# WKV inversion in packed 128x64 tiles, and in-step tiles kept in the conv layer's down products only

## The reference

```python
def step(state, inp):                       # wkv7_scan, 16 heads of 64, in both directions
    r_t, w_t, k_t, v_t, a_t, b_t = inp
    sa = einsum('bhvk,bhk->bhv', state, a_t)
    state = state * w_t[:, :, None, :] + sa[..., None] * b_t[:, :, None, :] + v_t[..., None] * k_t[:, :, None, :]
    y = einsum('bhvk,bhk->bhv', state, r_t)
    return state, y

def conv_ffn(h, w_up, conv_w, conv_b, w_down):
    u = h @ w_up                            # 1024 -> 2 * 2816
    acc = conv of width 3 over tokens
    gate, val = split(acc, 2)
    return (silu(gate) * val) @ w_down      # 2816 -> 1024
```

## Time and profile before

| | |
|---|---|
| median of three runs | 3595.13 us (3588.78 to 3596.03) |
| the profiled execution | 3587.22 us, span 3585.4 us, mean granted clock of TensorE 0.951 |
| TensorE busy | 3249.8 us, 91% of the span, 21000 matmul records |
| TensorE weight loads | 2580.9 us, 72% |
| VectorE busy | 2053.4 us, 57% |
| ScalarE busy | 1455.9 us, 41% |
| POOL busy | 725.8 us, 20% |
| DMA | 260.79 MB, 73 GB/s |

### The profile page before, as it was taken

One profiled execution on the slowest core, in us unless ns is written; L12 is line 12 of the kernel. 1 busy time (PEld: TensorE's weight loads), 2 busy tenths in 40 slices (PEclk: granted clock), 3 DMA queues, 4 the chain that ended last, 5 costly groups with the idle time before them and its releaser, 6 DMA issues. The chain is left out here.

```text
span 3585.4 us, 51130 instructions
## 1 busy us (share of the span) xinstructions
PE 3249.8 (91%) x21000; PEld 2580.9 (72%) x21000; DVE 2053.4 (57%) x2984; ACT 1455.9 (41%) x2418; POOL 725.8 (20%) x496
## 2 busy tenths in 40 slices
PE   8888999989878999989899997996888888889999
PEld 6656787868556888866588875765777777768887
DVE  6665634355764524356657375536677777547454
ACT  5444322234454212334644242445455544334332
POOL 1000302120001302020011012315454455201010
PEclk9999999999889999989999998997999999889999
DMA  4101333322003333320133232442000000023232
GB/s 144 41 1 65 106 95 93 99 71 88 10 8 99 95 95 94 95 71 7 48 96 105 83 96 79 156 173 69 22 25 25 25 25 34 7 88 100 95 93 84
DMA packets 82311, 260.79 MB, mean 73 GB/s; under 512 B 9632, under 2 KB 13216, under 8 KB 81696
## 3 DMA queue, kind: packets, MB, share of 16 engines
q1 hardware_dynamic: 71424, 236.02, 20.9%
q10 hardware_dynamic: 10656, 21.50, 1.6%
HBM read 236.51 MB, written 20.97 MB: 72 GB/s over the span
## 5 line engine op out<-in xcount | busy, mean ns | idle before, releaser
L1634 DVE TENSOR_TENSOR mlp_w_lo<-mlp_ring,mlp_w_hi 128x1024 fp32r<-128x1024 f32 (+1 forms) x211 | 251.6, 1193 | 616.9 <-ACT mlp_w_hi L1614 616.7
L1614 ACT ACTIVATE mlp_w_hi<-mlp_ring 128x1024 fp32r<-128x1024 f32 (+1 forms) x211 | 213.0, 1010 | 707.9 <-PE ps L1575 700.8
L1634 DVE TENSOR_TENSOR ffn_w_lo<-ffn_ring,ffn_w_hi 128x1024 fp32r<-128x1024 f32 (+3 forms) x172 | 225.7, 1312 | 459.8 <-ACT ffn_w_hi L1614 459.8
L1614 ACT ACTIVATE ffn_w_hi<-ffn_ring 128x1024 fp32r<-128x1024 f32 (+3 forms) x172 | 186.9, 1088 | 493.8 <-PE ps L1575 487.5
L1574 PE MATMUL ps<-mlp_more_parts,mlp_w_hi 128*128 128x512 f32 x952 | 377.5, 397 | 0.0
L1573 PE MATMUL ps<-mlp_more_parts,mlp_w_hi 128*128 128x512 f32 x760 | 312.1, 411 | 44.0 <-DVE mlp_w_lo L1634 29.1
L1573 PE MATMUL ps<-tiles_parts,mlp_w_hi 128*128 128x512 f32 x832 | 330.5, 397 | 8.0 <-issue 5.7
L1573 PE MATMUL ps<-ffn_x_parts,ffn_w_hi 128*128 128x512 f32 x792 | 312.7, 395 | 26.3 <-DVE ffn_x_parts L2344 20.9
L1575 PE MATMUL ps<-tiles_parts,mlp_w_lo 128*128 128x512 f32 x832 | 328.2, 394 | 0.0
L1574 PE MATMUL ps<-ffn_x_parts,ffn_w_hi 128*128 128x512 f32 x792 | 309.9, 391 | 0.0
L1575 PE MATMUL ps<-ffn_x_parts,ffn_w_lo 128*128 128x512 f32 x792 | 309.8, 391 | 0.0
(11 more groups left out here) (494 smaller groups left out, 6857.2 us busy)
## 6 DMA issues: line engine op xcount, KB each, us to landing
ffn_ring<-in_w_ffn_up SPq DMA_DIRECT2D x88, 512.0 KB, 3.5
mlp_ring<-in_w_up SPq DMA_DIRECT2D x64, 512.0 KB, 3.5
mlp_ring<-in_w_down SPq DMA_DIRECT2D x64, 512.0 KB, 3.5
rwkv_keep<-ffn_ring ACTq DMA_DIRECT2D x64, 256.0 KB, 2.5
sq<-rwkv_keep SPq DMA_DIRECT2D x64, 256.0 KB, 2.9
ffn_ring<-in_w_ffn_down SPq DMA_DIRECT2D x16, 768.0 KB, 4.3
in_ring<-in_w_in SPq DMA_DIRECT2D x22, 512.0 KB, 3.5
mlp_ring<-in_w_in SPq DMA_DIRECT2D x22, 512.0 KB, 3.5
```

Of the source, the lines that this page charges most:

```text
L1614: nc.scalar.activation(w.w_hi[:, n % SPLIT, 0:width], w.ring[:, n % RING, 0:width], ACT.Copy).then_inc(s["w_hi_ready"], 1)
L1634: nc.vector.tensor_tensor(w.w_lo[:, n % SPLIT, 0:width], w.ring[:, n % RING, 0:width], w.w_hi[:, n % SPLIT, 0:width].bitcast(F32), ALU.sub ...
```

## The change

The tiles of the inversion (M0, M2, X, XT, NM, T1) are packed by chunk: partition p = 64 u + token holds, per instance, the 64 columns of its own chunk u, so a tile is 128x64 per instance and 128x256 for four. `gram_a` writes them packed at once, as sixteen 64x64 products per t in the four quarters of the array. Masks get the same form (`eye` takes the identity's place), NM has four buffers instead of two and T1 memory of its own. `zv`, `wt` and `u0` work per chunk. Each turned tile leaves PSUM in one copy of 512 columns; tok_a goes. In `chain`, only a Linear with `in_step` does two tiles in step, with LATE = 4; only the conv layer's two down products per layer (12 and 10 k) have it.

```diff
-LATE = 2
+LATE = 4
...
-                if lin.parts == 1 and t == 0 and early > LATE and n + 1 < len(slots) and slots[n + 1][0].source is lin.source:
+                if lin.in_step and t == 0:
                     for first, last in ((0, early), (early, lin.ks)):
...
-        linears.append(added_to_x(nc, m, a[f"w_ffn_down{n}"], layer * DT, tiles, source))
+        linears.append(added_to_x(nc, m, a[f"w_ffn_down{n}"], layer * DT, tiles, source, in_step=True))
...
+PARTS_AHEAD = 4
...
-        M0 = sb("M0", [P, NT, 4, P])
-        M2 = sb("M2", [P, NT, 4, P])
+        M0 = sb("M0", [P, NT, 4, HD])
+        M2 = sb("M2", [P, NT, 4, HD])
...
-        tok_a = sb("tok_a", [P, 2, NT, P])
-        tok = sb("tok", [P, 2, 2, NT, 3, P])
+        tok = sb("tok", [P, 2, 2, NT, 4, P])
...
-        X = sb("X", [P, NT, 4, P])
-        XT = sb("XT", [P, NT, 4, P])
-        T1 = M2[:, 0:2, :, :]
-        NM = sb("NM", [P, 2, 4, P])
+        X = sb("X", [P, NT, 4, HD])
+        XT = sb("XT", [P, NT, 4, HD])
+        T1 = sb("T1", [P, 2, 4, HD])
+        NM = sb("NM", [P, PARTS_AHEAD, 4, HD])
...
+        def packed(i, n=1):
+            return slice(i * HD, (i + n) * HD)
...
+                def diagonals():
+                    return (0, 0), (1, 1), (0, 1), (1, 0)
...
-                    for d in range(2):
-                        for k in range(2):
-                            for hh in range(2):
-                                lo = half(hh)
+                    for k in range(2):
+                        for d in range(2):
+                            for hh, u in diagonals():
+                                lo, at = half(hh), packed(2 * t + u)
                                 lhsT, rhs = (A[lo, d, at], BK[lo, c % 2, 0, d, at]) if k == 0 else (BK[lo, c % 2, 1, d, at], A[lo, d, at])
-                                mm = nc.tensor.matmul(m.ps[:, 4 + hh, (2 * k + d) * P:(2 * k + d + 1) * P], lhsT, rhs, start=True, stop=True)
+                                mm = nc.tensor.matmul(m.ps[half(u), 4 + hh, packed(2 * k + d)], lhsT, rhs, start=True, stop=True,
+                                                      skip_group_check=True)
...
-                            mm = nc.tensor.matmul(m.ps[chunk, t % 2, at], NM[chunk, u % 2, i, chunk], XT[chunk, t, i, chunk], start=True, stop=True,
-                                                  skip_group_check=True)
+                            mm = nc.tensor.matmul(m.ps[chunk, t % 2, packed(i)], NM[chunk, u % PARTS_AHEAD, i, :], XT[chunk, t, i, :],
+                                                  start=True, stop=True, skip_group_check=True)
...
-                    for t, inst, d, e, at, _ in each(pair):
-                        mm = nc.tensor.matmul(m.ps[:, 2 + pair, at:at + HD], M2[:, t, inst, :], tok[:, c % 2, d, t, KIND_V, e], start=True, stop=True)
+                    for t, inst, d, e, at in each(pair):
+                        for chunk in (half(0), half(1)):
+                            mm = nc.tensor.matmul(m.ps[chunk, 2 + pair, at:at + HD], M2[chunk, t, inst, :], tok[chunk, c % 2, d, t, KIND_V, e],
+                                                  start=True, stop=True, skip_group_check=True)
...
-                    for t, inst, d, e, _, at in each(pair):
-                        mm = nc.tensor.matmul(m.ps[e, pair, at:at + P], tok_a[:, d, t, e], XT[:, t, inst, :], start=True, stop=True)
+                    for t, inst, d, e, _ in each(pair):
+                        for u in range(2):
+                            mm = nc.tensor.matmul(m.ps[e, u, packed(2 * t + d)], tok[half(u), c % 2, d, t, KIND_A, e], XT[half(u), t, inst, :],
+                                                  start=True, stop=True, skip_group_check=True)
...
-                    nc.scalar.activation(flat(tok[:, c % 2, d, t, :, :]), m.ps[:, n % 2, 0:3 * P], ACT.Copy).then_inc(s["turned_taken"], 1)
-                    nc.scalar.activation(tok_a[:, d, t, :], m.ps[:, n % 2, 3 * P:4 * P], ACT.Copy).then_inc(s["turned_taken"], 1)
+                    nc.scalar.activation(flat(tok[:, c % 2, d, t, :, :]), m.ps[:, n % 2, :], ACT.Copy).then_inc(s["turned_taken"], 1)
...
-                def wt_taken(c, pair):
-                    act.wait_ge(s["wt_ready"], 2 * c + pair + 1)
+                def wt_taken(c, u):
+                    act.wait_ge(s["wt_ready"], 2 * c + 2)
...
-                    pool.wait_ge(s["ma_ready"], 8 * c + 2 * t + 2)
+                    pool.wait_ge(s["ma_ready"], 8 * c + 2 * t + 1)
...
-                    if u >= 2:
-                        pool.wait_ge(s["inner_ready"], u - 1)
+                    if u >= PARTS_AHEAD:
+                        pool.wait_ge(s["inner_ready"], u - PARTS_AHEAD + 1)
...
-                    for hh in range(2):
-                        for k, (into, name) in enumerate(((M0, "after"), (M2, "before"))):
-                            scores = m.ps[:, 4 + hh, 2 * k * P:2 * (k + 1) * P].rearrange("p (d n) -> p d n", d=2)
-                            ins = nc.vector.tensor_tensor(into[:, t, 2 * hh:2 * hh + 2, :], scores, spread(mask(name), 2), ALU.mult)
-                        ins.then_inc(s["ma_ready"], 1)
+                    for k, (into, name) in enumerate(((M0, "after"), (M2, "before"))):
+                        scores = m.ps[:, 4:6, packed(2 * k, 2)].rearrange("p h (d n) -> p h d n", d=2)
+                        over = spread(mask(name), 4).rearrange("p (h d) n -> p h d n", h=2)
+                        dst = into[:, t, :, :].rearrange("p (h d) n -> p h d n", h=2)
+                        nc.vector.tensor_tensor(dst, scores, over, ALU.mult).then_inc(s["ma_ready"], 1)
```

More of the change, by code:

```diff
@@ L72 @@
 BANDS2_W = 3 * P
-RMASKS, RMASKS_W = columns(("after", P), ("before", P), ("upto", P), ("pair", P), ("merge", RW_LEVELS * P))
+RMASKS, RMASKS_W = columns(("after", HD), ("before", HD), ("upto", P), ("pair", HD), ("eye", HD), ("merge", RW_LEVELS * HD))
 def constants():
@@ L116, in constants, with table @@
     r = np.zeros((P, RMASKS_W), np.float32)
-    chunk = i // RW_CHUNK == j // RW_CHUNK
-    r[:, RMASKS["after"]:RMASKS["after"] + P] = chunk & (i > j)
-    r[:, RMASKS["before"]:RMASKS["before"] + P] = chunk & (i < j)
-    r[:, RMASKS["upto"]:RMASKS["upto"] + P] = chunk & (i <= j)
-    r[:, RMASKS["pair"]:RMASKS["pair"] + P] = (i // 2 == j // 2) & (i > j)
+    r[:, RMASKS["upto"]:RMASKS["upto"] + P] = (i // RW_CHUNK == j // RW_CHUNK) & (i <= j)
+    i, j = i % RW_CHUNK, np.arange(HD)[None, :]
+    def table(name, ones, level=0):
+        r[:, RMASKS[name] + level * HD:RMASKS[name] + (level + 1) * HD] = ones
+    table("after", i > j)
+    table("before", i < j)
+    table("pair", (i // 2 == j // 2) & (i > j))
+    table("eye", i == j)
     for level in range(RW_LEVELS):
@@ L124, in constants @@
         same = i // (2 * w) == j // (2 * w)
-        r[:, RMASKS["merge"] + level * P:RMASKS["merge"] + (level + 1) * P] = same & (i % (2 * w) >= w) & (j % (2 * w) < w)
+        table("merge", same & (i % (2 * w) >= w) & (j % (2 * w) < w), level)
     return {"consts": c, "masks": m, "bands1": b1, "bands2": b2, "rmasks": r}
@@ L1471, with __init__ @@
 class Linear:
-    def __init__(self, weights, base, tiles, ks, rhs, arrived, parts=1, after_first=None, on_act=None, on_dve=None, on_pool=None, last=0, source=None):
+    def __init__(self, weights, base, tiles, ks, rhs, arrived, parts=1, after_first=None, on_act=None, on_dve=None, on_pool=None, last=0, in_step=False):
         self.weights, self.base, self.tiles, self.ks, self.parts = weights, base, tiles, ks, parts
         self.rhs, self.arrived, self.after_first = rhs, arrived, after_first
-        self.source = source or self
+        self.in_step = in_step
         self.on_act, self.on_dve, self.on_pool, self.last = on_act, on_dve, on_pool, last
@@ L1753, in first_steps, with added_to_x @@
     return steps_of(lambda parts, eng, s, t: parts.act(eng, s, t)), steps_of(lambda parts, eng, s, t: parts.dve(eng, s, t))
-def added_to_x(nc, m, weights, base, ks, source, then=None, parts=1):
+def added_to_x(nc, m, weights, base, ks, source, then=None, parts=1, in_step=False):
     def on_dve(dve, s, lin, t):
@@ L1771, in on_pool @@
             then.pool(pool, s, t)
-    lin = Linear(weights, base, DT, ks, source.rhs, source.arrived, parts, None, on_act, on_dve, on_pool, last=1 if then else 0)
+    lin = Linear(weights, base, DT, ks, source.rhs, source.arrived, parts, None, on_act, on_dve, on_pool, last=1 if then else 0, in_step=in_step)
     if then:
@@ L1973, in in_projection @@
     act, dve = taken(y, vec[:, V1["b_in"]:V1["b_in"] + NIN], "p_biased", False)
-    return [first, Linear(a["w_in"], layer * NIN, NIN, DT, normed.rhs, normed.arrived, 1, {t: beside(t) for t in range(NIN)}, act, dve, last=2, source=first)]
+    return [first, Linear(a["w_in"], layer * NIN, NIN, DT, normed.rhs, normed.arrived, 1, {t: beside(t) for t in range(NIN)}, act, dve, last=2)]
 def qkv_product(nc, m, a, normed, y, prep):
@@ L2692, in seed @@
```

(17 more changed lines are left out.)

39 lines of the change are left out of this document (17 added, 22 removed).

## The result

The kernel after takes 3413.47 us (median of 4 runs, 3411.77 to 3414.22) against 3595.58 us: a ratio of 0.9495, 95% interval 0.9478 to 0.9511. Its profiled execution has a span of 3412.3 us, 173.1 less than before. Run again later beside another set of runs of before (3588.27 us), the same kernel took 3417.25 us, a ratio of 0.9518 (0.9505 to 0.9531); so 0.2% is indeed what a measurement can tell. The forecast was 3455 us, its range ended at 3425: the gain was 182 us, the forecast 140, and the range missed it by 12. The profiled execution of before lies 8 us under the median of its runs (3587.2 against 3595.6), that of after within 1 us of its own, so the spans show 9 us less of a gain than the medians.

The account below looks back on a forecast made before the run. TensorE was taken to bound most of the kernel, POOL the merge's first half with VectorE close behind. 3587.2 - 124 (WKV stage) - 16 (products) = 3447 us, standing for a median of 3455; range 3425 to 3502.

Parts of the forecast that it names:

- 1. Merge: WKV stage's merges, packed to 256 columns: 10.9 us less in each of six, 10 in the first, 4.5 in the last.
- What is late next: VectorE: In the merge, VectorE's queue sets the length once POOL's parts are halved: 30.5 us instead of 41.4.
- by which neighbours overlap: In the merge's VectorE sum, 0.06 us per instruction taken off for overlap, 3 us: 28.9 becomes 26.
- Rival 2: In the merge, VectorE isn't late because its long operations shorten with POOL's: merge 27.5 us, total 3434; chance 0.20.
- 2. Around the merge: Rest of a WKV iteration, bound by TensorE: seeds 1.8, zv and u0 3.7, copy 0.1, together 5.6 us less.
- gram_a: I take 0, by the nearest row: Score matrices before the merge: 32 quarter records at 0.029 us take 0.93 against 0.9 us, so nothing won.
- wt: nothing: The wt product around the merge: 32 records in 2.02 us become 64 in 1.9, so no gain.
- 0.45 if four quarters run together: Lower bound in us for gram_a's records of one tile; over four tiles 1.8 us won.
- 3. In step: Products outside the WKV stage: in step only in the down products, about 16 us less, ends 0 and 25.
- rival 4: In the products, the lateness that going in step covered is worth its stops: costs 5 us, 3476 us; chance 0.06.
- 1 (fixed costs of narrow operations): In the merge, 256 columns on POOL and in transposes cost nearly what 512 do: merge 35.5, total 3493 us; chance 0.20.
- 3 (quarter products in turn do not overlap): In gram_a, zv, wt and u0, 320 records at 0.115 us take 36.8 us per iteration: total 3669 us; chance 0.04.

Follow-up runs that it names:

- x4: Kernel after with the four reciprocals of a merge on VectorE replaced by memsets of constants: 3406.32 us, 0.9501 of before.
- x7: Kernel after with eight buffers for POOL's masked parts, the first four made ahead of its scale work: 3400.55 us, 0.9471 of before.
- x3: Kernel after with score-matrix and wt products reordered, first the two diagonal quarters, then the other two: 3421.48 us, 0.9547 of before.
- x9: Kernel after with R scores and outputs' sums also packed into the four quarters: 3385.47 us, 0.9442 of before.
- x1: Kernel before with only the change of `chain`, no tiles in step but in the down products: 3559.37 us, 0.9925 of before.
- x8: Kernel after with the first two tiles of the qkv product in step again, last 2 k left over: 3420.54 us, 0.9531 of before.
- x12: Kernel after with the last 2 k instead of 4 left over in the down products: 3416.20 us, 0.9521 of before.
- x2: Kernel after with the old `chain`, so the packed WKV stage alone: 3449.50 us, 0.9622 of before.
- x5: Kernel after, unchanged, run again beside other variants on the same chip: 3417.25 us.

## Why the prediction missed

Between the spans the forecast is 33 us short of the gain: 19 in the stretches between merges, 12 in the products, 2.5 in the rest of the stage, nothing in the merges. The other 9 us of the 42 by which the medians differ come from the 7.9 us that the sum added for the median of before, and which after did not have.

**1. Merge: the time right by luck, the reason wrong.** Every size but one was near: transposes 0.43, copies 0.38, parts 0.73 to 0.81 for 0.70, and the merges gave 79.9 us as forecast. But the step "What is late next: VectorE" fell. x4 took 5.8 us out of its queue in each merge and won 0.4. What makes 31.9 us out of TensorE's own 26.6 is a stop of 1.7 us for POOL, one of 1.0 us for U, and the lower clock behind them (records of 1.81 and 1.07 us, 1.5 us in sum); x7 took the first and the third away. I had summed POOL's work to 19.3 us over the whole merge and taken it for no bound. It is busy 12.25 of the first 14.2 us, with five scale operations of 1.3 to 1.7 us among the parts: a sum over a stage hides a queue that is full in its first half. The floor of TensorE was 26.6 us, not 25.3. The sum had an error of its own too: the 33.2 us of VectorE in the earlier trace rows are counted without overlap already, so the 3 us "by which neighbours overlap" were taken off twice, and without that the same steps give 33.5 us for a merge, not 30.5. And the forecast gave the clock no term, though up to 29 of the 79.9 us came by it. That the sums agree is luck: the first merge fell by 8.9 us (forecast 10), the last by 5.5 (4.5), the others by 10.2 to 12.0 (10.9). Rival 2 (VectorE not late, 27.5 us) was right in its condition and wrong in its time.

**2. Around the merge: the step that failed.** Seeds, zv, u0 and the copy of a turned tile (0.83 us of wait, forecast 0.8) came as forecast. "gram_a: I take 0, by the nearest row" and "wt: nothing" did not. I priced both at 0.029 us per record by L2715, in which only two quarters ever work. These two use all four, and then 64 records of wt take 1.0 us (0.016 each) and the 32 of a tile 0.63. Of gram_a I had the bound itself, "0.45 if four quarters run together", and took the row with two. 0.9 + 4 x 0.36 = 2.3 us per iteration, eight times 19 us. With 5.2 for the terms that were forecast at 5.6 (zv 1.7, u0 1.65, seeds 1.7, the copy 0.1) this makes 7.5 of the 7.7 by which most stretches fell. x3 shows for gram_a that the order of quarters does 0.28 of the 0.36 us per tile, x9 that it holds for other products; for wt it is argued from its rate, and x3, which put wt's quarters in the other order too, slowed wt and u0 by 0.2 us only. Without these 19 us the time would have lain inside the range. Another 4 us of the 57.7 were no gain of the change: in the profiled execution of before one zv took 7.09 us instead of 3.79, at a granted clock of 0.50 though the longest stop in the 6 us ahead of it was 0.96 us, and the stretch 48.1 instead of 44.1; in x1, with the same stage, no zv did, though other stretches there are longer (302.6 us in sum).

```profile
3042.66 7.09 PE L2745 MATMUL ps<-heads_tok,heads_M 128*128 128x64 f32 x32
```

```profile
3042.60:3049.80 7.20, 7.20 (x34) 7.14 (x34) 4.29 (x8) 1.24 (x3) 3.65 (x3) 0.50 0.01 2
```

**3. In step: a term mis-sized.** 28 us for 16; x1 shows them alone. By the traces the qkv product gave 7.4 us for the 4 forecast: its stop had a stretch at half clock behind it, which x8 brings back (6.8 us). The two down products of 12 k gave 2.5 and 2.3 us for 0.8 each; in both, in before, k steps of 1.28 us followed the stop of 2.16, but x12 has the stop without them, so this part is a matter of the moment. The RWKV inputs gave 5 us for two stops of 2.45 in sum: in before the tiles behind the stop at 2237.22 begin with two k of 0.74 to 0.80 us instead of 0.68, in after they do not; why, I have not tried. Losses were as small as forecast (0.3 us at each ffn_up for 0.7) except in w_out and MLP of the first layer, where stops of 1.11 and 1.16 us went and nothing was won, -0.5 us in sum; rival 4 holds there. A stop was counted at its length, and the clock behind it at nothing.

**Rivals.** 1 (fixed costs of narrow operations) fell with 0.43, 0.38 and 0.81 us. 3 (quarter products in turn do not overlap) was the opposite of what happened. That the Trainium skill's rule on the port pair of VectorE and GpSimd (SBUF — State Buffer, its table of terms) would hand VectorE time back is borne out in one row, 0.91 for 1.71 us; the same operation takes 0.69 us in both kernels the last time, where POOL is idle, which is a better witness than the L3088 of the forecast. It decided nothing, as x4 shows. The Trainium skill's rule that a change of tiling mode drains TensorE (TensorEngine Tiling (Array Packing), Key Properties) shows as 0.34 us from 2734.07 to 2734.41, where the 16 records before took 0.29: 0.05 us per change, too little to see in the sum.

**Still open.** What brings the clock down: stops of 2.16 us did it in before and not in x12, the same two stops did it in three merges of after and not in two, and before zv no stop over 0.96 us stood. The same clock is most of why kernels with the same first mixers differ there: x1 and x2 lose 6 to 7 us against the profiled execution of before and x5 2 to 3, and from 170 to 330 us the granted clock was 0.90 in before, 0.87 in x1, 0.86 in x2 and 0.88 in x5, by an estimate 5, 6 and 3 us.

## What to carry to other kernels

Price 64x64 products by the fullest quarter of the array: a quarter began a record every 0.058 us here, which is 0.029 us per record where the neighbours in the queue use two quarters and 0.015 where they use four, accumulating or not. Ask of every engine what its queue holds in each third of a stage, not over the whole. And count a stop of TensorE with what may follow it: here 4.2 us of standing still cost 7 in place, though the whole kernel took only 3 us longer. Before a gain or a wait is put down to an engine, compare stretches of the same granted clock.

## What the runs showed of the hardware

Four quarters of 64x64 ran at twice the rate of two (x9: eight records in 0.117 us, the merge: sixteen in 0.46). After the stop of 4.21 us the granted clock was 0.50 for 4.8 us in before and 0.53 in x8; after 1.67 us of stop in a merge it was 0.72 for 6 us in three merges of after and stayed at 1.00 in two; in x12 it stayed at 1.00 after 2.16 us.
